# Both products of an MLP by seven block products, with the first one's results parked in DRAM

## The reference

```python
h = rms_norm(x, g_mlp[l])                                        # 1024 x 1024
f = jnp.square(jax.nn.relu(jnp.einsum("bsd,df->bsf", h, w_1[l])))  # w_1: 1024 x 4096
x = x + jnp.einsum("bsf,fd->bsd", f, w_2[l])                     # w_2: 4096 x 1024
return rms_norm(x, g_final)
```

## Time and profile before

| | |
|---|---|
| median of 3 runs | 2386.34 us (2386.21 to 2386.46) |
| the profiled execution | 2386.64 us |
| its span, first to last instruction | 2384.8 us, so 1.8 us lie around it |
| mean granted TensorE clock | 0.998 |
| PE busy | 2369.0 us of the span |
| DVE busy | 1549.4 us |
| ACT busy | 902.7 us |
| POOL busy | 84.4 us |

### The profile page before, as it was taken

How to read it: one execution, slowest core, us unless ns; L and a number is a source line. 1 busy time by engine, 2 the same in 40 slices (tenths; PEclk the granted TensorE clock), 3 DMA queues, 4 the chain that set the end, 5 groups by cost and what they waited for, 6 DMA issues and landing times.

```text
span 2384.8 us, 26302 instructions
## 1 busy us (share of the span) xinstructions
PE 2369.0 (99%) x10688; PEld 1923.4 (81%) x10688; DVE 1549.4 (65%) x2162; ACT 902.7 (38%) x1370; POOL 84.4 (4%) x103
## 2 busy tenths in 40 slices
PE   9999999999999999999999999999999999999998
PEld 7778688687788888888888888888888877888887
DVE  8899599598779744466655665534667544462377
ACT  6552442443512632333433343332343232222364
POOL 0000000000000000011111111000000000000000
PEclk9999999999999999999999999999999999999999
DMA  4201112012031112312212211112211111211222
GB/s 139 58 23 54 62 36 76 27 45 76 29 104 45 45 45 72 96 49 62 58 32 62 62 47 42 58 45 73 81 45 48 45 45 45 52 51 49 71 87 82
DMA packets 228321, 138.43 MB, mean 58 GB/s; under 512 B 15968, under 2 KB 219104, under 8 KB 228200
## 3 DMA queue, kind: packets, MB, share of 16 engines
q1 hardware_dynamic: 228200, 136.75, 19.5%
HBM read 127.78 MB, written 8.95 MB: 57 GB/s over the span
## 4 chain that ended last, share of the span: by engine, by line
PE 87%; DVE 8%; ACT 4%; issue 1%; DMA 0%; SPq 0%; DVEq 0%; ACTq 0%
PE bank L669 27%; PE bank L671 26%; PE bank L670 26%; PE bank L782 3%; DVE q_all L2872 1%; DVE v L2028 1%; PE bank L1055 1%; ACT whi L1193 1%; DVE uw L2638 0%; PE bank L1037 0%; PE bank L971 0%; DVE uc L2280 0%; DVE wlo L1899 0%; ACT un_hi L1209 0%; ACT bank L1419 0%
## 5 line engine op out<-in xcount | busy, mean ns | idle before, releaser
L669 PE MATMUL bank<-h_hi,whi 128*128 128x512 f32 x1984 | 780.2, 393 | 1.5 <-DVE h_lo L1921 1.1
L671 PE MATMUL bank<-h_hi,wlo 128*128 128x512 f32 x1984 | 773.0, 390 | 0.0
L670 PE MATMUL bank<-h_lo,whi 128*128 128x512 f32 x1984 | 772.6, 389 | 0.0
L669 PEld LDWEIGHTS bank<-h_hi,whi 128*128 128x128 f32 x1984 | 372.6, 188 | 83.0 <-DVE h_lo L1921 2.2
L670 PEld LDWEIGHTS bank<-h_lo,whi 128*128 128x128 f32 x1984 | 372.7, 188 | 79.5 <-issue 2.9
L671 PEld LDWEIGHTS bank<-h_hi,wlo 128*128 128x128 f32 x1984 | 372.7, 188 | 78.0
L1899 DVE TENSOR_TENSOR wlo<-raw,whi 128x1024 fp32r<-128x1024 f32 (+2 forms) x233 | 272.4, 1172 | 141.2 <-ACT whi L1193 139.6
L1193 ACT ACTIVATE whi<-raw 128x1024 fp32r<-128x1024 f32 (+2 forms) x233 | 232.5, 1004 | 269.0 <-PE bank L671 220.2
L2373 DVE SCALAR_TENSOR_TENSOR tmp<-bank,factor 128x512 f32<-128x512 f32 x64 | 44.2, 690 | 89.8 <-PE bank L671 89.8
L782 PE MATMUL bank<-v,gate_w 128*128 128x512 f32 x224 | 97.4, 592 | 0.0
L2392 DVE TENSOR_TENSOR x<-x,bank 128x512 f32<-128x512 f32 x96 | 65.7, 685 | 47.3 <-ACT bank L1500 46.4
(11 more groups left out here) (406 smaller groups left out, 3675.3 us busy)
## 6 DMA issues: line engine op xcount, KB each, us to landing
raw<-in_w_in SPq DMA_DIRECT2D x90, 512.0 KB, 3.7
raw<-in_w SPq DMA_DIRECT2D x40, 512.0 KB, 3.9
raw<-in_w_b_out SPq DMA_DIRECT2D x16, 384.0 KB, 3.1
raw<-in_w SPq DMA_DIRECT2D x24, 256.0 KB, 2.7
raw<-in_w SPq DMA_DIRECT2D x48, 128.0 KB, 2.2
raw<-in_w_out SPq DMA_DIRECT2D x11, 512.0 KB, 3.4
raw<-in_w_a_out SPq DMA_DIRECT2D x8, 512.0 KB, 3.8
raw<-in_w_o SPq DMA_DIRECT2D x8, 512.0 KB, 3.9
```

Source lines behind the costliest of these rows:

```text
L669: pe.matmul(target, lh, rh, start=start, stop=False, skip_group_check=True)
L670: pe.matmul(target, lh, rl, start=False, stop=False, skip_group_check=True)
L671: last = pe.matmul(target, ll, rh, start=False, stop=stop and point is not None, skip_group_check=True)
```

## The change

It does the following.

- The first product uses the seven-product scheme too. Work is now cut in units: `UP` = 16 units for `w1` (a pair of output tiles j and j+4 by all 8 input tiles), then 4 x `DOWN` = 12 units for `w2` (3 groups of 8 hidden tiles). A unit has seven products of 4 x 3 = 12 matmuls each (`HK` = 4), in the old order (`ORDER`, 196 turns; unit w's products 1, 5, 2, 6 stand in window w, its 7, 3, 4 in window w+1).
- The hidden results do not stay in SBUF. For units 0 to 11, DVE forms from the four squares (b11, b12, b21, b22) the combinations t1 to t4; SP stores seven 128x512 tiles to `ff_dram`. Units 12 to 15 store the four squares only. When a group of `w2` units comes near, `load_piece` reads its combinations back, two DMAs for each of seven names, ACT and DVE split them (`c_part`, `c_low`).
- Weights are loaded as two 128x1024 tiles a unit (`load_unit`), two units in `unit_raw`. DVE makes four sums a unit (`first_sums`, `later_sum`) instead of GpSimd, in place in the raw tiles. A product's left side is a granule of 128x512, high and low (`ghi`, `glo`, six rooms), made 4 or 5 turns ahead (`LEAD`).
- The norm's factor comes from eight narrow matmuls (`x1_stat`), a root and a reciprocal of 128x8, and eight transposing matmuls (`spread`).
- Of the `w2` columns, the last 8 hidden tiles stay plain; they are read back from DRAM (`load_ff`), the first two output tiles together (`tiles_together`).

```diff
-PIECE = 4
-PIECES = 6
+UP = D_FF // (2 * P)
+DOWN = FC - 1
+UNITS = UP + 4 * DOWN
+HK = DT // 2
+ORDER = [(w - late, n) for w in range(UNITS + 1) for n, late in ((1, 0), (5, 0), (7, 1), (2, 0), (3, 1), (6, 0), (4, 1))
+         if 0 <= w - late < UNITS]
+GRANULES = 6
+LEAD = (5, 5, 4, 4, 4, 5, 5)
...
+            def load_unit(u, *parts):
...
+                        for n in ((6, 3), (7, 4))[m]:
+                            w.wait_ge(*at("g", u - 2, n))
+                    sp.dma_start(unit_raw[u % 2][m][:].rearrange("p (k c) -> p k c", k=DT), tiles_of(rows, row0, DT, columns[m], P)).then_inc(
...
+            def load_piece(u, name):
...
+                w.wait_ge(*at("unit", u, AT_STEP[name]))
+                for m in range(2):
...
+                    sp.dma_start(c_in[name][:, 2 * m:2 * m + 2, :], ff_dram[first:first + 2, dram_row(name)].rearrange("k p t -> p k t")).then_inc(
...
```

```diff
-            def x1_sum(half):
-                w.wait_ge(*at("square_total", DT - 1, half))
-                pe.matmul(sum_banks[half][:], ones_sq[:], squares[half][:], start=True, stop=True, skip_group_check=True).then_inc(
+            def x1_stat():
...
+                for t in range(NT):
+                    last = pe.matmul(stat_bank[:, t:t + 1], squares[t // 4][:, t % 4 * P:(t % 4 + 1) * P], ones[:, 0:1],
...
-            for e in range(PIECES):
-                for j in TURNS:
-                    block_product(number["w1", e, j], ("w1", e, j, 0), h2, "h2", 0, used=False)
...
+            for u, n in ORDER:
+                product(u, n)
+                if (u, n) == (0, 2):
+                    x1_stat()
+                if (u, n) == (0, 7):
+                    for half in range(2):
+                        w.wait_ge(*at("x1_r"))
+                        spread(0, half, "x1_factor", sum_banks[half])
...
+            for half in range(2):
+                tiles_together([("w2", FC - 1, j) for j in range(2)], half, ff, f"ff{FC - 1}", order=FF_TILES)
+            for j in range(2, DT - 2):
...
+            def first_sums(u):
+                a11, a12, a21, a22, total = parts_of(u)
+                w.wait_ge(*at("unit_in", u, 1))
...
+                dve.tensor_tensor(total, a21, a22, ALU.add).then_inc(*did(("sum", u, 5)))
+                w.wait_ge(*at("unit_in", u, 0))
+                dve.tensor_tensor(a21, a11, a21, ALU.subtract).then_inc(*did(("sum", u, 7)))
...
+            for k, (u, n) in enumerate(ORDER):
+                granules(k + lead(k))
+                if n == 1:
+                    last_difference(u - 2)
...
+                if n == 6:
+                    three_differences(u - 1)
+                    third_seed(u)
...
+                new_combos(u, n)
...
-                pool.tensor_tensor(s1, a21, a22, ALU.add).then_inc(*up("pool_done"))
-                pool.tensor_tensor(s3, a11, a21, ALU.subtract).then_inc(*up("pool_done"))
-                w.wait_ge(*now("pool_done", 1))
-                pool.tensor_tensor(s2, s1, a11, ALU.subtract).then_inc(*up("pool_done"))
-                w.wait_ge(*now("pool_done"))
-                pool.tensor_tensor(s4, a12, s2, ALU.subtract).then_inc(*up("pool_done", ("sums", e, c)))
```

More of the change, by code:

```diff
@@ L387, in build_program @@
[L387 to L391, removed]
+        ff_in = sb("ff_in", "h", 0, [P, DT, 2 * SEQ])
@@ new lines, in build_program @@
+        COMBO_AT = {"b11": ("g", 0), "t1": ("g", 16 * KB), "b21": ("g", 32 * KB), "t2": ("g", 48 * KB),
+                    "b22": ("h", 0), "t3": ("h", 16 * KB), "t4": ("h", 32 * KB)}
+        c_hi, c_lo = ({name: [sb(f"c_{kind}_{name}{p}", where, o + 4096 * p + 2048 * m, [P, HALF], F32R) for p in range(HK)]
+                       for name, (where, o) in COMBO_AT.items()} for m, kind in enumerate(("hi", "lo")))
+        c_in = {name: sb(f"c_in_{name}", where, o, [P, HK, SEQ])[:, :, HALF:SEQ] for name, (where, o) in COMBO_AT.items()}
@@ new lines, in load_ff @@
+            def load_ff(n, half):
+                j = FF_TILES[n][0]
+                name, first = ("b21" if j >= HK else "b11", "b22" if j >= HK else "b12")[half], WHOLE + j % HK
+                for v in range(first, first + 2):
+                    w.wait_ge(*at("stored", v, name))
+                sp.dma_start(ff_in[:, j:j + 2, SEQ + half * HALF:SEQ + (half + 1) * HALF],
+                             ff_dram[first:first + 2, dram_row(name)].rearrange("k p t -> p k t")).then_inc(
+                    *landed(f"ff_in{2 * n + half}", ("ff_in", j, half), ("ff_in", j + 1, half)))
@@ L1542, in scalar, with first_seed @@
-            for j in range(DT):
-                ahead(number["w1", FC - 1, j, "end"] + 2)
-                for half in range(2):
-                    t = tmp[half]
-                    w.wait_ge(*at("relu", FC - 1, j, "end", half))
-                    act.activation(t[:], t[:], ACT.Square).then_inc(*did(("relu_square", FC - 1, j, "end", half)))
-                    w.wait_ge(*now("act_done"))
-                    w.wait_ge(*at("m", PIECES - 1, 3, 4))
-                    split_hi(("ff_hi", j, half), ff[0][j][:, cut(half)], t[:])
+            def first_seed(u):
+                w.wait_ge(*at("unit", u, 1))
+                w.wait_ge(*at("free", *earlier["first", u]))
+                act.activation(bank("first", u)[:], bank("chain", u)[:], ACT.Copy).then_inc(*did(("first_seed", u)))
@@ L1551, in scalar @@
+            for n in range(1, 4):
+                ff_part(n, 0)
+            for n in range(1, 4):
+                ff_part(n, 1)
             for j in range(DT - 2):
@@ L2324, in vector, with x1_total, parts_of @@
                     split_mix(j)
+            def x1_total(j, half):
+                total = sum_banks[half] if j < DT - 1 else squares[half]
+                w.wait_ge(*at("squares", j, half))
+                dve.tensor_tensor(total[:], sum_banks[half][:], squares[half][:], ALU.add).then_inc(*did(("square_total", j, half)))
+            def parts_of(u):
+                one, two = unit_raw[u % 2]
+                return one[:, cut(0)], one[:, cut(1)], two[:, cut(0)], two[:, cut(1)], first_sum[u % 2][:]
@@ L2473, in vector, with room_for @@
[L2473 to L2480 removed]
+            def room_for(u, name):
+                if (before := last_stored(u, name)):
+                    w.wait_ge(*at(*before))
@@ new lines, in last_difference, with third_seed @@
+            def last_difference(u):
+                if not 0 <= u < WHOLE:
+                    return
+                w.wait_ge(*at("ff", u, "b21"))
+                w.wait_ge(*at("ff", u, "t2"))
+                difference(u, "t4", tmp[tmp_of(u, "b21")], tmp[tmp_of(u, "t2")])
+            def third_seed(u):
+                w.wait_ge(*at("unit", u, 6))
+                w.wait_ge(*at("fifth_copy", u))
+                w.wait_ge(*at("free", *earlier["third", u]))
+                dve.tensor_tensor(bank("third", u)[:], bank("chain", u)[:], fifth[u % 2][:], ALU.add).then_inc(*did(("third_seed", u)))
```

799 lines of the change are left out of this document (480 added, 319 removed).

## The result

The changed kernel takes 2368.36 us (median of 4 runs, 2362.53 to 2370.78), the kernel before on the same chip 2386.40: ratio 0.992, interval 0.9901 to 0.9939. It is faster, as forecast, but by 18.0 us and not by 39.1. The time lies above the range.

A forecast was written before the change was run, and what follows sets the result against it. PE was taken to bound the kernel, so time falls with the number of matmuls: 2386.6 - 43.5 + 2.4 (start) + 1.5 (group changes) + 0.5 (end) = 2347.5, given as 2347.3 us for the median; range 2343 to 2362.

The forecast's parts named there:

- What is removed: Matmuls of the MLP: 192 fewer at a pitch of 0.2267 us, 43.5 us less if PE keeps its pitch.
- Steady windows: Windows of seven turns, 19.0 us on PE: DVE's 13.6 us and ACT's 9 us of work both fit.
- Its cost is thus nothing: Weight load released by product 4's low part lands at turn 3.4, DVE reaches `first_sums` at 3.5; cost 0.
- hand replay: One steady window followed in turns: third_seed done at 7.3, needed at 9; DVE idles 1.3 turns a window.
- If that cover went (landing 2 us later), the seed's slack would take it: Weight load in steady windows: a landing 2 us later would be absorbed by third_seed's slack of 1.7 turns, 4.6 us.
- The start: Behind `wo`: waits for two seeds and `x1_r` (1.4) plus new matmuls, 4.1 us, less the old sums' 1.7: +2.4.
- The changes of group: Three changes: DVE falls behind but slack carries it, no stall, 2 us to spare; 0.5 each for small misses, +1.5.
- The end: Last `ff` tiles read back after the last products, asked for 8.2 us or more ahead: +0.5, bounds 0 and 3.
- Rival 1: DVE too slow in the starts and group changes, at 0.69 and handoffs in full: 2359; chance 0.15.
- Rival 2: Read-backs land late at the three group changes, DVE and ACT waiting in order: 3 to 9 us, about 2352; chance 0.10.
- Rival 3: Weight loop closes if a late load makes `first_sums` hold third_seed; 10.7 us called harmless; 2391 and more; chance 0.03.
- Rival 4: Gain eaten to nothing by a missed wait in every window, 1.5 us x 28: 2386; chance 0.02.

The follow-up runs named there:

- three repairs: Changed kernel with the bank ring started at bank 4, ACT's squares behind the next turn's high parts, and the second weight tile loaded in two halves: 2343.24 us, 0.9819.
- the second trace: The changed kernel measured again with no edit, for the spread and another trace: 2366.92 us, ratio 0.9915.
- the ring's edit: One line on the changed kernel puts the ring of PSUM banks four positions on for the plain part and all behind it: 2359.14 us, 0.9885 alone.

## Why the prediction was wrong

- **What is removed: right.** 192 matmuls fewer on the MLP, and 2352 by 0.2267 is the MLP's length wherever the loop is open (3.8 us beside it with three repairs, all at the start).
- **Steady windows, "Its cost is thus nothing": this step failed**, at 14.3 us. The operations and their price were right: 13.6 us foreseen a window, and 19.64 less 3.66 for ACT and 2.37 for the load leaves 13.6. What the hand replay missed is that ACT's queue has `square` ahead of a high part. It says "Both fit, but order decides", and then gives turns for DVE only and replays no order of ACT against it. The waits take 3.7 us of DVE's margin of 5.4 (19.0 less 13.6; the replay's own 1.3 idle turns are 3.5 us, less still); the exposed landing, 2.4 here and 2.7 on the mean, no longer fits in the rest. The sentence "If that cover went (landing 2 us later), the seed's slack would take it" was wrong in kind too: a slack takes a delay once, a loop adds it each time round.
- **A step that was not there: 6.8 us.** The change removes requests from the bank ring, which moves every later user to another bank. One had to wait 5.1 us for `h3_part` and brought the granted clock to 0.50 behind it. The cost is 7.9 against the 274.1 us that this stretch takes at best; 1.1 came back by luck, since the fall of the clock that the kernel before has there stayed out. The prediction named a fallen clock as a danger, but at the start.
- **The start: right** in mechanism, and near in size by errors that cancel: 3.5 us lost against 4.1, 3.8 with the tenths. The wait for `x1_r` cost 0.6 and not 1.4. The eight narrow matmuls moved the next start by 1.7 us (1041.86 to 1043.56) and not by 1.1: the row with x8 in the earlier trace rows is four matmuls of two records each, not eight. The first product also starts 0.9 later in this trace than before, 1033.3 for 1032.4, but at 1032.5 in the second trace and between 1032.1 and 1033.7 in the others; that is not the change's.
- **The changes of group:** 1.3 against 1.5 is near by chance. All of it is at one of the three and on ACT, and with three repairs nothing is lost there: it was the closed loop's, and the replay's "No stall" was right. **The end:** nothing lost against 0.5.
- **The rivals.** Rival 1 has its kind of wait in the wrong place: seeds are late in the steady windows, not in the starts and group changes. Its price by full durations was wrong: independent operations of 0.68 to 0.69 us still start 0.60 to 0.61 apart (1215.93 and 1216.54), so none costs its full duration here either. The Trainium skill's "VectorE: DVE Perf Modes", TRN2 errata, has a fixed latency exposed between instructions, 151/0.96 ns of its (N+151)/0.96. By an estimate from that formula some 0.07 to 0.08 us of this 0.16 is in the pitch of 0.60 to 0.61, since 512/0.96 ns are 0.53: the exposure is there in part, where the prediction says that the trace does not agree on it. Rival 2's late read-backs did not happen. Rival 3 had the right loop, and closed it by landings after 10.7 us; they take 3.9, and DVE's own waits closed it. The 10.7 is also wrong by itself: it counts from the release to the seed's last harmless moment once, and not round the loop. The 19 operations without their waits take 12.0 us, so a landing after 7.0 would close it. Rival 4, a missed wait in every window at 1.5 us, is nearest to what happened: 12 windows of 28, at 1.2 us each.

With 3.5, 14.3, 1.3 and 0 in the MLP, 0.9 ahead of it and 6.8 behind: 2386.6 - 43.5 - 3.5 (what the stretch of 580.2 lost before) + 0.9 + 19.1 + 1.1 (tenths and rounding) + 6.8 = 2367.5; the profiled execution took 2367.3. For the kernel with three repairs the same sum is 2386.6 - 43.5 - 3.5 + 0.1 (its first product starts at 1032.5) + 3.8 = 2343.5; its median is 2343.2.

## What to carry to other kernels

Where a buffer's release starts a load whose data the releasing engine needs, add up the whole way round (landing exposed, operations, each handoff between two in-order queues) and compare it with the other engine's period; shares of busy time can't show it, one more operation in the loop does. Replay the second queue against the first: an ACT instruction that waits for DVE, ahead of one that DVE waits for, cost two operations here, 1.22 us. When requests are taken out of a rotation of buffers, look at who gets which buffer behind the change, however far.

## What the runs showed of the hardware

A stop of TensorE of 5.1 us was followed by 5.7 us at granted clock 0.50. Every changed kernel here without the ring's edit shows such a stop of 5.1 to 5.6 us and a clock of 0.50 to 0.55 over the 5 us behind it, and the kernels with the edit have neither at that place; it made the wait half as dear again. A fall to 0.50 does not need such a stop: behind eight narrow matmuls and 0.26 us without one, the trace of the kernel before and six others have some 3 us of it, and six traces with the same matmuls have none. It costs 1.1 us, so two traces can differ by that much with nothing changed there.

VectorE's operations of 128x512 in float32 last 0.69 us and start 0.60 to 0.61 apart. A narrow float32 matmul, with a right side of one column, has two records in these traces, and eight of them moved the next start by 1.7 us. Within one execution a load that landed late (5.9 us from issue to use, for 3.9) made PE's matmul 2.25 us late while the loop was closed.
